# Prompt mLSTM: where the causal bound enters the decay weights, and from where ScalarE reads them

## The reference, cut to what matters

```
b = cumsum(log sigmoid forget gate);  ih = input gate
dmat = where(causal, b[l] - b[s] + ih[s], -inf)
m_t = max(b[l] + m_state, max_s dmat[l, s])
w_intra = exp(dmat - m_t[l])
a = w_intra * (q_l . k_s)
num = sum_s a v_s + exp(b[l] + m_state - m_t) * (C_state q_l)
den = max(|sum_s a + exp(...) * (n_state q_l)|, exp(-m_t));  h = num / den
C_new = sc * C_state + sum_l wk_l v_l k_l^T   (and n_new in the same way)
```

## Time and profile before

| | us |
|---|---|
| median of 3 runs | 1029.63 |
| profiled execution | 1025.48 |
| its span (first to last instruction) | 1023.7 |
| TensorE matmul busy in the span | 908.0 (89%) |
| VectorE busy | 518.5 (51%) |
| ScalarE busy | 372.0 (36%) |
| GpSimd busy | 99.3 (10%) |
| mean granted TensorE clock, share of full speed | 0.908 |

### The profile page before, as it was taken

How to read it: one execution, slowest core, us unless ns; L and a number is a source line. 1 busy time by engine, 2 the same in 40 slices (tenths; PEclk the granted TensorE clock), 3 DMA queues, 4 the chain that set the end, 5 groups by cost and what they waited for, 6 DMA issues and landing times.

```text
span 1023.7 us, 19861 instructions
## 1 busy us (share of the span) xinstructions
PE 908.0 (89%) x7903; PEld 813.9 (79%) x7903; DVE 518.5 (51%) x1116; ACT 372.0 (36%) x740; POOL 99.3 (10%) x164
## 2 busy tenths in 40 slices
PE   5999988999889888784879859999999999999993
PEld 5888877778775555573659749999999999999982
DVE  4622345523336567556553365667667667222225
ACT  4332344645224556110121164433444344212115
POOL 2012313353410000300100000000000000000000
PEclk9989999999995799855569879999999999999997
DMA  8257777776650000001043102322222222222212
GB/s 295 83 153 241 256 243 238 225 212 216 211 207 1 1 2 1 2 1 61 33 188 133 62 1 84 100 86 83 83 100 86 84 83 90 80 84 90 73 34 88
DMA packets 54191, 112.46 MB, mean 110 GB/s; under 512 B 6969, under 2 KB 32346, under 8 KB 53650
## 3 DMA queue, kind: packets, MB, share of 16 engines
q1 hardware_dynamic: 45656, 89.06, 26.5%
q0 software_dynamic: 6528, 17.83, 5.7%
q10 hardware_dynamic: 1914, 4.29, 1.2%
HBM read 105.54 MB, written 12.40 MB: 115 GB/s over the span
## 4 chain that ended last, share of the span: by engine, by line
PE 76%; DVE 9%; issue 6%; ACT 4%; DMA 3%; POOLq 1%; POOL 1%; SPq 0%; ACTq 0%; DVEq 0%
PE q L1687 29%; PE q L1685 26%; PE q L2004 2%; DMA arena<-in_pool 2%; PE q L2032 2%; PE q L2022 2%; PE q L2193 2%; PE q L2194 2%; PE q L2162 1%; PE q L2111 1%; PE q L1749 1%; POOLq L490 1%; ACT whi L947 1%; PE q L1737 1%; DVE xt L1353 1%
## 5 line engine op out<-in xcount | busy, mean ns | idle before, releaser
L471 DVE TENSOR_TENSOR wring_r<-wring,whi_r 128x1024 fp32r<-128x1024 f32 (+1 forms) x101 | 120.5, 1193 | 334.3 <-ACT whi_r L468 334.2
L468 ACT ACTIVATE whi_r<-wring 128x1024 fp32r<-128x1024 f32 (+1 forms) x101 | 104.3, 1033 | 334.9 <-PE q L1687 308.2
L1687 PE MATMUL q<-xt_r,whi_r 128*128 128x288 f32 x552 | 166.4, 301 | 0.0
L1685 PE MATMUL q<-xt_r,whi_r 128*128 128x256 f32 x552 | 156.8, 284 | 0.0
L1685 PE MATMUL q<-arena_r,whi_r 128*128 128x256 f32 x440 | 136.2, 310 | 20.0 <-DVE xt_r L471 11.6
L1687 PE MATMUL q<-arena_r,whi_r 128*128 128x288 f32 x440 | 133.0, 302 | 0.0
L1687 PE MATMUL q<-arena_r,wring_r 128*128 128x288 f32 x440 | 132.7, 302 | 0.0
L1685 PE MATMUL q<-arena_r,wring_r 128*128 128x256 f32 x440 | 125.5, 285 | 0.0
L1685 PE MATMUL q<-mixt_r,whi_r 128*128 128x256 f32 x400 | 113.2, 283 | 10.5 <-DVE xt_r L471 10.5
L1687 PE MATMUL q<-mixt_r,whi_r 128*128 128x288 f32 x400 | 119.6, 299 | 0.0
L1685 PEld LDWEIGHTS q<-arena_r,whi_r 128*128 128x128 f32 x440 | 85.0, 193 | 27.2 <-issue 19.5
(11 more groups left out here) (405 smaller groups left out, 1569.3 us busy)
## 6 DMA issues: line engine op xcount, KB each, us to landing
wring<-in_w_up SPq DMA_DIRECT2D x42, 512.0 KB, 3.4
wring<-in_w_in SPq DMA_DIRECT2D x27, 512.0 KB, 5.1
arena<-in_pool SPq DMA_DIRECT2D x64, 192.0 KB, 3.6
arena<-in_pool POOLq DMA_DIRECT2D x64, 192.0 KB, 4.1
wring<-in_w_down SPq DMA_DIRECT2D x24, 448.0 KB, 3.2
arena<-in_pool SPq DMA_DIRECT2D x64, 64.0 KB, 2.2
arena<-in_pool POOLq DMA_DIRECT2D x64, 64.0 KB, 2.5
wring<-in_w_out SPq DMA_DIRECT2D x8, 512.0 KB, 9.5
```

Source lines behind the costliest of these rows:

```text
L468: return eng.activation(out, src, ACT.Copy)
L471: return eng.tensor_tensor(out, src, hi.bitcast(F32), ALU.subtract)
L1685: pe.matmul(out[:, 0, 0:HALF], w, x[:, 0:HALF], start=(kk == 0 and n == 0), stop=(end and n == 2))
L1687: mm = pe.matmul(out[:, 1, 0:HALF + NS], w, x[:, HALF:NT], start=(kk == 0 and n == 0), stop=(end and n == 2))
```

## The change

The decay step of VectorE goes. Behind each exponent product, TensorE adds the product of the identity with the table `causal`, repeated four times over the bank, into the same bank, so that forbidden places get -1e30 added. ScalarE reads the two banks itself, takes the exponential and writes `whi_f`. The semaphore `ml_x` goes; TensorE waits for `ml_w` where it waited for `ml_x`, and ScalarE waits for `ml_d` (the banks are filled) and, from chunk 2 on, for `ml_v` of two chunks back, whose values product read the same half of `whi_f`.

```diff
             for c in range(QT):
-                act.wait_ge(ml_x, c + 1)
-                act.activation(whi_f[:, c % 2, :], whi_f[:, c % 2, :], ACT.Exp).then_inc(ml_w, 1)
+                act.wait_ge(ml_d, c + 1)
+                if c >= 2:
+                    act.wait_ge(ml_v, c - 1)
+                act.activation(whi_f[:, c % 2, :], q4[0].rearrange("p b c -> p (b c)"), ACT.Exp).then_inc(ml_w, 1)
...
-            def decay(c):
-                dve.wait_ge(ml_d, c + 1)
-                dve.tensor_tensor(by_block(whi_f[:, c % 2, :]), by_block(q4[0].rearrange("p b c -> p (b c)")),
-                                  causal.unsqueeze(1).broadcast_to([128, H, 128]), ALU.min).then_inc(ml_x, 1)
...
-            decay(0)
             carry(0)
             products(0)
             for c in range(QT):
-                if c + 1 < QT:
-                    decay(c + 1)
                 normed(c)
...
                 if c >= 1:
                     pe.wait_ge(ml_ce, c)
-                    pe.wait_ge(ml_x, c)
+                    pe.wait_ge(ml_w, c)
                 for q in range(2):
-                    mm = pe.matmul(bank[q], gl[:, token_rows(c)], rows[:, c % 2, 512 * q:512 * q + 512],
-                                   start=True, stop=True)
+                    pe.matmul(bank[q], gl[:, token_rows(c)], rows[:, c % 2, 512 * q:512 * q + 512], start=True, stop=False)
+                    mm = pe.matmul(bank[q], ident, causal.unsqueeze(1).broadcast_to([128, 4, 128]), start=False, stop=True)
                 mm.then_inc(ml_d, 1)
...
             def new_state(c):
                 pe.wait_ge(ml_wv, c + 1)
-                pe.wait_ge(ml_x, c + 1)
+                pe.wait_ge(ml_w, c + 1)
```

More of the change, by code:

```diff
@@ L404, in layer @@
         tok_v_ev, tok_k_ev = sem("tok_v_ev"), sem("tok_k_ev")
-        gl_set, ml_rc, ml_r, ml_d, ml_s, ml_x, ml_w, ml_a = (sem(n) for n in (
-            "gl_set", "ml_rc", "ml_r", "ml_d", "ml_s", "ml_x", "ml_w", "ml_a"))
+        gl_set, ml_rc, ml_r, ml_d, ml_s, ml_w, ml_a = (sem(n) for n in (
+            "gl_set", "ml_rc", "ml_r", "ml_d", "ml_s", "ml_w", "ml_a"))
         ml_st, ml_ce, ml_v, ml_cb, ml_n, ml_wv = (sem(n) for n in ("ml_st", "ml_ce", "ml_v", "ml_cb", "ml_n", "ml_wv"))
```

## The result

The kernel after takes 1043.53 us (median of 4 runs, 1042.42 to 1046.34) beside 1030.01 for the one before (4 runs, 1028.43 to 1034.73). So the change costs 13 to 15 us. The forecast had the sign and 1038.2 us; the measured time lies 1 us above the upper end of its range.

What follows compares the result with a forecast made beforehand. The prediction held that VectorE waits for TensorE in the mLSTM loop, so work added to TensorE costs time. +10.1 us for added products less the removal, -1.5 for the clock, gave +8.6: 1038.2 us, range 1032.0 to 1042.5.

Steps and rivals of the forecast that it cites:

- What bounds the stage: Four-chunk mLSTM loop: VectorE, 3.98 us idle before normed in the last chunk, waits for TensorE's value product.
- Removed, -0.16 us, in chunk 0 alone: Decay step is on the path only in chunk 0: ScalarE's exponential, 1.06 us, replaces its 1.22.
- the bounds of 1.0 and 1.2: ScalarE's exponential reading PSUM: 1.0 us lower end, 1.19 upper end, 1.06 taken.
- Added, on the chain in each chunk: Identity products behind exponent products: 1.73 us per chunk at 2.4 GHz, 3.40 at 1.2; with the removal +10.10 together.
- The weight loads of 0.19 us lie under the passes.: TensorE's added identity products: their weight loads are hidden, so only record spacing, 0.43 or 0.85 us, is charged.
- The clock, -1.5 us: TensorE's granted clock falls about as before; one value product of three runs at the upper level, -1.5 us.
- the held clock (1027.7): Rival: identity products keep TensorE at 2.4 GHz from chunk 2 to the last values; -1.9 us, chance 0.05.
- the clock held in part (1033.5): Rival: chunk 2 at the upper clock level, chunk 3 not; +3.9 us, chance 0.11.
- the hidden products (1029.5): Rival: added products cost nothing, as TensorE idles up to 3.76 us in a chunk; -0.2 us, chance 0.04.
- The colder one: Rival: longer loop puts the clock's first fall before chunk 1's exponents are through; +13.6 us, 1043.2, chance 0.12.
- twice the price as the upper bound: Identity product of 128 rows, 512 columns, fp32, in no row: bounded by 0 and twice the price; L2074's spacing taken.
- Adding the sum to the median: +8.6 us added to the runs' median, 1029.63, giving 1038.2; the profiled execution lay 4.15 us below that median.

Runs made afterwards that it cites:

- e5: Changed kernel without the identity products: no decay step, ScalarE reads PSUM, causal bound left out; 1030.90 us, 1.0003 of the kernel before.
- e6: Kernel before with VectorE's decay step done twice in chunks 1 to 3; 1030.27 us, 0.9996 of the kernel before.
- e7: Kernel before with the identity products added, decay step and waits kept; 1046.33 us, 1.0142 of the kernel before.
- e2: Changed kernel with each chunk's products grouped: both 40-row exponent products, then both 128-row identity products; 1034.73 us, 1.0064 of the kernel before.
- e3: Changed kernel with the identity product cut to 40 of its 128 rows, most of the causal bound left out; 1045.01 us, 1.0157 of the kernel before.
- e1: The changed kernel run again, nothing altered; 1043.91 us, 1.0150 of the kernel before.
- e9: Changed kernel with both identity products of a chunk ahead of both exponent products; 1035.32 us, 1.0058 of the kernel before.
- e10: Changed kernel with bank 1's identity and exponent products ahead of the wait for the carry, then bank 0's; 1033.85 us, 1.0032 of the kernel before.
- e11: Kernel before with VectorE's carry and scores-times-weights product moved into the middle of normed; 1023.14 us, 0.9931 of the kernel before.
- e4: Changed kernel with identity and causal table copied to bf16 beforehand, same product order; 1038.02 us, 1.0088 of the kernel before.
- e12: Kernel before with the carry in the middle of normed and bank 1's exponent product ahead of the wait for the carry; 1013.86 us, 0.9835 of before.
- e8: Kernel before with bank 1's exponent product put ahead of the wait for the carry; 1023.94 us, 0.9936 of the kernel before.

## Why the prediction was wrong, point by point

- **What bounds the stage**: right. VectorE waits for TensorE there; e5 and e6 are ratios of 1.0003 and 0.9996.
- **Removed, -0.16 us, in chunk 0 alone**: right, -0.26 in e5. ScalarE's exponential from PSUM took 1.02 us, inside the bounds of 1.0 and 1.2.
- **Added, on the chain in each chunk**: the place was right, and e7 shows that it is the whole loss within the intervals. The size was not. This is the step that failed: "The weight loads of 0.19 us lie under the passes." They do between products of the same 40 rows, which is all that the earlier trace rows show; between 40 and 128 rows they do not (e2, e3): a product takes 1.05 us in place of 0.86 at 2.4 GHz and 2.00 in place of 1.71 at 1.2 GHz. The trace of the kernel before already had one such place, where the value product of chunk 0 (128 rows) follows the exponent product (40 rows). Its weight side idles 0.76 us there, against 0.24 between the 40-row records:

```profile
424.28 1.95 PEld L2111 LDWEIGHTS q<-arena,whi 128*128 128x128 f32 x16 [0.76 <-issue]
```

The traces of before and after, chunk by chunk:

| | forecast | before | after | difference |
|---|---|---|---|---|
| chunk 0, exponents to new state | +1.57 | 3.45 | 5.50 | +2.05 |
| chunk 1, exponents to values | +1.73 | 1.88 | 4.09 | +2.21 |
| chunk 0's values to normed | 0 | 2.17 | 1.93 | -0.24 |
| chunk 2, exponents to values | +3.40 | 4.24 | 9.89 | +5.65 |
| chunk 3, exponents to values | +3.40 | 5.28 | 9.89 | +4.61 |
| clock | -1.5 | | | in the rows above |
| sum | +8.6 | | | +14.3 |

The 16 added records at 0.43 and 0.85 us make 10.3 us, as the forecast had them. Chunk 3 ran at 1.2 GHz on both sides, so its 4.61 less 3.41 is the price of the exposed loads and of the overlap that the last exponent pass had with the carried products: 1.2 us; chunks 0 and 1 give 0.5 each in the same way, and 1.2 is taken for chunk 2: 3.4 us in all.

- **The clock, -1.5 us**: wrong in sign in this pair of profiles. In chunk 2, 1.2 us for loads and 3.4 for passes leave +1.04: before, part of its exponents still ran at 2.4 GHz, after, none did. With the -0.24 of chunk 0's values it is +0.8. In this profile the clock held through chunk 1, as argued, but it fell in the idle time behind it just the same (436.8), and every added product of chunk 2 then ran at the lower level. That the added height held it is not shown: it held as long in e5, without any identity product (15.0 us into the stage), and not in e7, with all of them (8.3 us). 3.4 for loads and 2.3 for the clock are the 5.7 us between forecast and trace.
- **The rivals**: the held clock (1027.7), the clock held in part (1033.5) and the hidden products (1029.5) are out. The colder one has the right time, 1043.2, by another way: its clock was to fall before chunk 1's exponents were through, and in the profiles of after and e1 it did not (in that of e7, with the same products, it did). That its number is near is chance, as it had no term for the loads. The range was drawn from the clock alone and left no room for a second cost per product, though the text had named twice the price as the upper bound of a product never seen; that bound was not carried into the range.
- **Adding the sum to the median**: the profiled execution of before lay 4.5 us below the median of 1030.01, that of after 1 us below its own, so the two profiles differ by 17.1 us and the medians by 13.5. The stage accounts for 14.4 of the former.

## What to carry to other kernels

Work moved from an engine that waits to the one it waits for was paid in full here, however idle the mean share of the first and however long the second stands still elsewhere; look at what ends the idle time, and whether the new work is behind it in the queue. Price an added product with the neighbours that it will have, the row heights above all; look in the trace that you have for a place where the rows change, as there was one here; and carry the upper bound of an operation that the trace has never shown into the range. Where TensorE idles for a buffer, ask which half of its next work does not need that buffer, and what the engine that frees it could do later: this brought 16 us where the planned change cost 13.

## What the runs showed of the hardware

- Back to back, fp32 products of 128x512 whose weights use the same rows start 0.86 us apart at 2.4 GHz and 1.71 at 1.2 GHz, whether 40 rows (e3) or 128 (the pairs of e2 and e9). Between 40 and 128 rows, in either direction, the next load waits for the end of the product before: 1.05 and 2.00 us. The Trainium skill's page "TensorE: Matmul & The Clock Gate", section "The mechanism", says in its list that weight loads overlap running products only where the row groups differ, and in its text that a load into the background weight buffer is pulled ahead too. Here loads of equal rows were hidden, against the list as it stands, and those of overlapping, unequal rows were not; the measurement decides. No run here shows which buffer a load went to.
- Two 128-row fp32 products behind each other, begun at 1.2 GHz, were followed by 2.4 GHz in three of four chunks (both late ones of e2, at 443.3 and 460.4 us, and one of two in e9, at 442.7). The same products in turn with 40-row ones, 8 us without a gap, were not in any of the six late chunks of after, e1 and e7. The clock rose in other places too, in after under the scores and the new state (453.8 and 474.3).
- Where the clock first fell does not follow the height of the products alone. Counted from the first product of the stage, in one profile each: 17.2, 18.5, 16.9, 17.2 and 16.9 us in after, e1, e2, e9 and e10, but 8.3 in e7, all with the 128-row fp32 products; without them 3.2 in e3, 6.5 in e11, 6.9 in e4, 8.3 in before and in e6, but 13.7 in e12, 13.8 in e8 and 15.0 in e5.
- The exponential of 128x1024 took 1.02 us from PSUM (after, e5) against 1.06 from SBUF (before).
